# List entries of a routed expert loop loaded one step ahead and copied on the chip: one Trainium2 core, two-layer encoder with mixture of experts

## The reference

```python
for i in range(DEPTH):
    ...
    h = rmsnorm(x, norm_ffn_g[i])
    x = x + hierarchical_moe(h, ...)   # top-1 of 4 groups, top-2 of its 8 experts
...
def expert_block(args):
    xb, e = args                       # up to 128 tokens of expert e
    hid = jax.nn.silu(xb @ w_gate[e]) * (xb @ w_up[e])
    return hid @ w_down[e]
```

## Time and profile before

| | us |
|---|---|
| median of 3 runs | 2135.43 |
| lowest and highest of them | 2134.26, 2157.36 |
| the profiled execution, its own time | 2135.17 |
| span of the profiled execution | 2133.3 |

### The profile page before, as it was taken

How to read it: one execution, slowest core, us unless ns; L and a number is a source line. 1 busy time by engine, 2 the same in 40 slices (tenths; PEclk the granted TensorE clock), 3 DMA queues, 4 the chain that set the end, 5 groups by cost and what they waited for, 6 DMA issues and landing times.

```text
span 2133.3 us, 31870 instructions
## 1 busy us (share of the span) xinstructions
PE 2004.4 (94%) x9518; PEld 1668.4 (78%) x9518; DVE 1574.5 (74%) x1886; ACT 1360.6 (64%) x1734; POOL 284.7 (13%) x313
## 2 busy tenths in 40 slices
PE   7999999999979999999999969998799999999991
PEld 6888778888867888888888758887688888888871
DVE  4334453426558989999999866777799999999986
ACT  3442243434337888888888855315588888888873
POOL 1000000000031222122112100001312112222110
PEclk9999999999979999999999979998899999999996
DMA  7331223323367999999999964233989999999976
GB/s 281 99 99 69 80 86 101 93 88 128 139 197 286 368 363 381 384 391 370 379 379 379 367 244 162 99 149 129 276 331 377 379 380 383 376 379 388 395 296 254
DMA packets 166743, 560.12 MB, mean 263 GB/s; under 512 B 31472, under 2 KB 32720, under 8 KB 164512
## 3 DMA queue, kind: packets, MB, share of 16 engines
q1 hardware_dynamic: 138816, 510.72, 64.1%
q0 software_dynamic: 25424, 39.56, 5.3%
q10 hardware_dynamic: 2448, 9.14, 1.2%
HBM read 541.94 MB, written 51.97 MB: 278 GB/s over the span
## 4 chain that ended last, share of the span: by engine, by line
PE 48%; DMA 30%; issue 9%; DVE 6%; POOLq 3%; ACT 2%; POOL 2%; SPq 0%; ACTq 0%; DVEq 0%; PEldq 0%
DMA y_rows<-big,metas 17%; PE bank L572 15%; PE bank L573 15%; PE bank L574 15%; DMA metas<-lists 11%; POOLq L504 2%; PE bank L652 1%; POOL big L507 1%; DVE big L1333 1%; PE bank L800 1%; DVE w_lo L1325 1%; PE bank L641 1%; DVE big L1582 1%; DVE bank L1578 1%; DVE x_res L1352 1%
## 5 line engine op out<-in xcount | busy, mean ns | idle before, releaser
L572 PE MATMUL bank<-w_hi,a_hi 128*128 128x512 f32 x1944 | 773.3, 398 | 15.7 <-DVE w_lo L1325 9.3
L574 PE MATMUL bank<-w_hi,a_lo 128*128 128x512 f32 x1944 | 760.8, 391 | 0.0
L573 PE MATMUL bank<-w_lo,a_hi 128*128 128x512 f32 x1944 | 758.6, 390 | 0.0
L1325 DVE TENSOR_TENSOR w_lo<-raw,w_hi 128x1024 fp32r<-128x1024 f32 x372 | 452.8, 1224 | 358.7 <-ACT w_hi L947 337.5
L947 ACT ACTIVATE w_hi<-raw 128x1024 fp32r<-128x1024 f32 x372 | 393.0, 1060 | 453.9 <-PE bank L574 438.6
L1325 DVE TENSOR_TENSOR w_lo<-big,w_hi 128x1024 fp32r<-128x1024 f32 x530 | 620.8, 1220 | 28.8 <-ACT w_hi L947 21.3
L947 ACT ACTIVATE w_hi<-big 128x1024 fp32r<-128x1024 f32 x530 | 547.7, 1064 | 104.2 <-PE bank L574 98.8
L572 PEld LDWEIGHTS bank<-w_hi,a_hi 128*128 128x128 f32 x1944 | 367.0, 189 | 91.6 <-DVE w_lo L1325 12.2
L574 PEld LDWEIGHTS bank<-w_hi,a_lo 128*128 128x128 f32 x1944 | 366.1, 188 | 79.2
L573 PEld LDWEIGHTS bank<-w_lo,a_hi 128*128 128x128 f32 x1944 | 366.7, 189 | 72.3
L1325 DVE TENSOR_TENSOR a_lo<-bank,a_hi 128x512 fp32r<-128x512 f32 x227 | 147.6, 684 | 58.7 <-ACT a_hi L947 51.9
(11 more groups left out here) (185 smaller groups left out, 1606.4 us busy)
## 6 DMA issues: line engine op xcount, KB each, us to landing
big<-in_w_gate SPq DMA_DIRECT2D x260, 512.0 KB
big<-in_w_up SPq DMA_DIRECT2D x254, 512.0 KB, 6.7
raw<-in_w_down SPq DMA_DIRECT2D x244, 512.0 KB, 6.7
raw<-in_a_w_in SPq DMA_DIRECT2D x64, 512.0 KB, 3.9
raw<-in_a_w_out SPq DMA_DIRECT2D x32, 512.0 KB, 3.2
big<-y_rows SPq DMA_DIRECT2D x16, 1024.0 KB, 7.0
big<-in_w_down SPq DMA_DIRECT2D x16, 512.0 KB, 9.8
raw<-in_b_w_in SPq DMA_DIRECT2D x16, 512.0 KB, 4.2
```

The costliest lines, as they stand in the source:

```text
L572: pe.matmul(dst, left_hi, right_hi, start=first, stop=False)
L573: pe.matmul(dst, left_hi, right_lo, start=False, stop=False)
L574: return pe.matmul(dst, left_lo, right_hi, start=False, stop=last)
L1325: return nc.vector.tensor_tensor(dst, src, f32(hi), ALU.subtract)
```

## The change

`metas` stays, and two buffers of the same form, `ahead_g` and `ahead_s`, are put into columns of `cols` that held the bias of the first mixer. The DMAs load into these; a GpSimd `tensor_copy` of 128x4 int32 then fills `meta_g` or `meta_s`. The load for the gather of item i+2 is issued right behind the gather of item i+1; the load for the scaling of item i+1 is issued right behind the scatter of item i, and its copy is made when that scatter has landed. ACT waits for the copy instead of the DMA (the counts change from 16 per load to 1 per copy). Three more groups of edits only rename: `stored`, `table`, `xc_act`, `xc_dve` and `summed` become one semaphore for both layers, with counts that run on.

```diff
+        ahead_g, ahead_s = cols[:, 0:4].bitcast(I32), cols[:, 4:8].bitcast(I32)
...
+                def load_ahead(i, dst, landed):
+                    b = block_of(i)
+                    pool.dma_start(dst, lst[:, bass.ds(b, 1), :].rearrange("p b w -> p (b w)")).then_inc(landed, 16)
+
                 def gather(i):
 
-                    b = block_of(i)
                     pool.wait_ge(M.x_full, i)
                     waited()
-                    pool.dma_start(meta_g, lst[:, bass.ds(b, 1), :].rearrange("p b w -> p (b w)")).then_inc(M.meta_g, 16)
-                    pool.wait_ge(M.meta_g, 16 * (i + 1 - FIRST))
+                    pool.wait_ge(M.ahead_g, 16 * (i + 1 - FIRST))
+                    waited()
+                    nc.gpsimd.tensor_copy(meta_g, ahead_g).then_inc(M.meta_g, 1)
+                    pool.wait_ge(M.meta_g, i + 1 - FIRST)
                     waited()
                     gather_rows(0, xg, M.gathered)
 
-                def load_meta(i):
-                    b = block_of(i)
-                    pool.dma_start(meta_s, lst[:, bass.ds(b, 1), :].rearrange("p b w -> p (b w)")).then_inc(M.meta_s, 16)
+                def scale_by(i):
+
+                    pool.wait_ge(M.ahead_s, 16 * (i + 1))
+                    waited()
+                    nc.gpsimd.tensor_copy(meta_s, ahead_s).then_inc(M.meta_s, 1)
+                    pool.wait_ge(M.meta_s, i + 1)
+                    waited()
...
                 def scatter(i):
                     scatter_rows(i, meta_s, y_sb)
+                    load_ahead(i + 1, ahead_s, M.ahead_s)
                     pool.wait_ge(M.scattered, 16 * (i + 1))
                     waited()
+                    scale_by(i + 1)
...
-                load_meta(0)
+                load_ahead(0, ahead_s, M.ahead_s)
+                load_ahead(2, ahead_g, M.ahead_g)
+                scale_by(0)
                 load_gain(2 * L + 2, A["norm_mix_g"][1] if L == 0 else A["final_norm_g"])
                 gather(2)
...
+                load_ahead(3, ahead_g, M.ahead_g)
                 with pool.Fori(2, n - 1) as i:
                     gather(i + 1)
+                    load_ahead(i + 2, ahead_g, M.ahead_g)
                     scatter(i - 2)
-                    load_meta(i - 1)
                 scatter(n - 3)
-                load_meta(n - 2)
                 scatter_rows(n - 2, meta_s, y_sb)
                 scatter_rows(n - 1, meta_g, end_y)
...
-                    act.wait_ge(M.meta_s, 16 * (i + 1))
+                    act.wait_ge(M.meta_s, i + 1)
                     weighted_rows(y_sb, 2, meta_s)
```

More of the change, by code:

```diff
@@ L223, in encoder_trunk @@
         ROUTE = ["rw_ready", "x_t", "lg_full", "lg_read", "slots", "slot_oh", "first_full", "first", "weighted",
[L224 to L228, removed]
+                 "exps", "g_shifted", "e_shifted", "chosen", "ranked", "placed", "listed", "small", "second", "rows", "row_full", "table",
+                 "xc_act", "xc_dve", "summed"]
+        rt = sems("route", ROUTE, {"stored": HALVES})
+        MOE = ["hi", "lo", "used", "chain",
+               "meta_g", "ahead_g", "ahead_s", "gathered", "x_full", "x_hi", "x_lo", "silu", "hid",
                "h_full", "h_hi", "h_lo", "y_out", "meta_s", "scattered",
-               "added", "summed"]
-        m = [sems(f"moe{n}", MOE, {"raw": ROUND, "stored": HALVES}) for n in range(LAYERS)]
+               "added"]
+        m = [sems(f"moe{n}", MOE, {"raw": ROUND}) for n in range(LAYERS)]
         SU = 3 * 2 * KC
@@ L245, in copied @@
             if L == 0:
-                return m[L].xc_act, 2 * (t + 1)
-            return (m[L].xc_dve, 2 * (t + 1)) if t < HT else (m[L].xc_act, 2 * (t - HT + 1))
+                return rt.xc_act, 2 * (t + 1)
+            return (rt.xc_dve, 2 * (t + 1)) if t < HT else (rt.xc_act, 2 * TT + 2 * (t - HT + 1))
         block = ctx.enter_context(nc.Block())
@@ L326, in load_dn @@
                         .then_inc(landed if landed is not None else M.raw[GU + j], 16)
-                place_free = {0: lambda: sp.wait_ge(M.stored[0], 16),
-                              4: lambda: sp.wait_ge(M.stored[1], 16 * HT),
+                place_free = {0: lambda: sp.wait_ge(rt.stored[0], 16 * (L + 1)),
+                              4: lambda: sp.wait_ge(rt.stored[1], 16 * HT * (L + 1)),
                               5: lambda: sp.wait_ge(rt.first_full, HALVES * L + HALVES),
@@ L389, in moe @@
                 if L == 0:
-                    sp.wait_ge(M.table, 1)
+                    sp.wait_ge(rt.table, L + 1)
                     for grp in (2, 3):
@@ L863, in moe @@
                 h_transposes(1)
-                pe.wait_ge(M.table, 1)
+                pe.wait_ge(rt.table, L + 1)
                 n = pe.value_load(table[0:1, 0, TABLE - 1:TABLE], min_val=E - 2, max_val=ITEMS_MAX - 2) + 2
@@ L969, in raw_copy @@
                 for j in range(2):
-                    copy(xt[L][t][:, j * 512:(j + 1) * 512], bank[b + j][:, :]).then_inc(m[L].xc_act, 1)
+                    copy(xt[L][t][:, j * 512:(j + 1) * 512], bank[b + j][:, :]).then_inc(rt.xc_act, 1)
             def logits_copy(L, t, b):
@@ L1188, in moe @@
                         if L == 0:
-                            act.wait_ge(M.stored[1], 16 * HT)
+                            act.wait_ge(rt.stored[1], 16 * HT)
                             for i in range(4):
@@ L1214, in moe @@
                 round_(2, moe_raw, early_down)
-                act.wait_ge(M.table, 1)
+                act.wait_ge(rt.table, L + 1)
                 n = act.value_load(table[0:1, 0, TABLE - 1:TABLE], min_val=E - 2, max_val=ITEMS_MAX - 2) + 2
@@ L1232, in moe @@
                 act.wait_ge(M.used, ROUND * n + DN)
-                act.wait_ge(M.meta_g, 16 * (n - FIRST))
+                act.wait_ge(M.meta_g, n - FIRST)
                 weighted_rows(end_y, 4, meta_g)
@@ L1349, in add @@
                 dve.wait_ge(g.comb[t % COMBS], 16 * ((L * TT + t) // COMBS + 1))
-                nc.vector.tensor_tensor(two[:, 0, :], two[:, 0, :], two[:, 1, :], ALU.add).then_inc(M.summed, 1)
-                dve.wait_ge(M.summed, t + 1)
+                nc.vector.tensor_tensor(two[:, 0, :], two[:, 0, :], two[:, 1, :], ALU.add).then_inc(rt.summed, 1)
+                dve.wait_ge(rt.summed, TT * L + t + 1)
                 nc.vector.tensor_tensor(x_res[:, t, :], x_res[:, t, :], two[:, 0, :], ALU.add).then_inc(M.added, 1)
@@ L1731, in moe @@
                 round_(2, moe_raw, early_down)
-                dve.wait_ge(M.table, 1)
+                dve.wait_ge(rt.table, L + 1)
                 n = dve.value_load(table[0:1, 0, TABLE - 1:TABLE], min_val=E - 2, max_val=ITEMS_MAX - 2) + 2
```

14 lines of the change are left out of this document (7 added, 7 removed).

## The result

| us | before | after |
|---|---|---|
| median | 2142.22 (2132.96 to 2157.6, 15 runs) | 2123.56 (2119.72 to 2130.76, 15 runs) |
| profiled execution, span | 2133.3 | 2117.8 |

The medians lie 18.7 us apart, the two profiles 15.5 us.

A forecast was written before the change was run, and what follows sets the result against it. PE's own work was taken as the bound at 17.80 us a round, with stalls from late list entries on top. Terms -7.3, -4.6 and -2.1 summed to -14.0 us, from 2135.17 to 2121.2 us; range 2116 to 2131.

The forecast's parts named there:

- PE's own work takes 17.80 us a round, and the excess over it is what can be won: Expert-stage rounds in both layers: PE sets 17.80 us a round; only the stalls beyond that can go.
- -7.3, -4.6 and -2.1: Stalls expected to go, in us: layer 0's rounds, layer 1's rounds, and layer 1's tail behind the last x transposes.
- What is late first is meta_s: POOL's string ahead of `y_out`: the load of `meta_s` has 0.3 us of cover; moving it gives 7 us.
- pays only by making POOL's loop shorter ... PE gains nothing more from that: Load of `meta_g` a round ahead: takes 5.2 us off POOL's string, adds a copy, gives PE nothing more.
- the 3.16 us of issue: Late issue on POOL in layer 0's longest stall, with a scatter of 8.37 us; expected to fit the new cover.
- Room of POOL, about 6 us a round: POOL's loop after the change: 11.5 us and two copies against 17.80, so POOL waits about 6 us for `y_out`.
- Copies of 0.2 us, 0.3 with their wait: Two GpSimd copies of 128x4 a round: 0.2 us each, 0.3 with wait, 0.98 at most, hidden in POOL's idle time.
- DVE pays nothing: DVE beside the copies: 1.2 us free a round, 0.4 lost at 0.2 per copy, so cost taken as 0.
- Ahead of layer 1's loop, 0 between -1.5 and +2: New order of loads, copy, gain and gather before layer 1's loop: taken as 0, ends -1.5 and +2 us.
- Rival A: Copies held for whole DVE runs make POOL's loop 21.5 us: +215 us, 2336 us; chance 0.04.
- Rival B: Copies cost DVE more than its 1.2 us free a round: 2136 us, at the end 2167; chance 0.11.
- Rival C: Small load queued behind the scatter's packets, `meta_s` there at 22.9 us, half the gain: 2128 us; chance 0.08.

The follow-up runs named there:

- e1: Changed kernel with only the scaling's entries loaded ahead, the gather loading its own as before: ratio to the kernel before 0.9999, median 2145.87 us.
- e2: Changed kernel with only the gather's entries loaded ahead, the scaling's loaded behind the landed scatter: ratio to the kernel before 0.9922, median 2128.61 us.
- e8: Changed kernel with eight GpSimd memsets of 128x1024 ahead of each gather in layer 1's loop: its items 3 to 31 took 653.7 us against 498.4.
- e7: Changed kernel with four GpSimd memsets of 128x1024 ahead of each gather in layer 1's loop: its items 3 to 31 took 499.5 us against 498.4.
- e4: Changed kernel with eight more GpSimd copies of 128x4 a round, four ahead of each copy: ratio to the kernel before 0.9939, median 2134.25 us.

## Why the prediction was right or wrong

The forecast was 2121.2 us, 14.0 below the profiled execution of 2135.17, and the median of the changed kernel is 2123.56, inside the range. The profiles differ by 15.5 us, the ratio's interval gives 13 to 23. That the time itself came so near is in part luck: the forecast started near the median of three runs, 2135.43, and by 15 runs it is 2142.22; 14.0 below that would be 2128.2.

- *PE's own work takes 17.80 us a round, and the excess over it is what can be won:* right to the hundredth. -7.3, -4.6 and -2.1 came as they were summed, since no stall is left, and no round from item 3 on falls below 17.79.
- *"What is late first is meta_s", and the gather's load ahead "pays only by making POOL's loop shorter ... PE gains nothing more from that":* this step failed, though the sum did not show it. I had given the gather until 17.8 us and had not set its landing against that. e1 shows that when only `y_out` is relieved the gather takes over as what is late, and the timed runs gain nothing; e2 shows that the shorter string alone removes every stall. What was right in it is the arithmetic of the string, and the sentence that it happens to be as long as PE's round. That it "wanders" was the smaller part: most of the stalls stand behind the 3.16 us of issue, which the prediction had seen once and counted as the longest late case.
- *Room of POOL, about 6 us a round:* of the right size. In the changed kernel's round POOL idles 2.88 and 4.71 us. The sum had the scatter at 7.6 us, where it took 5.7, and the copies at 0.6 with their waits, where they took 1.7. 4.4 us of memsets are hidden and use the room up, as the scatter lands later with them; 8.9 are not.
- *Copies of 0.2 us, 0.3 with their wait:* a copy alone takes 0.18, but in the loop it took 1.13 (ahead of the gather) and 0.59 (behind the scatter) by the median. The prediction's sentence on the Trainium skill had this: by the page "SBUF — State Buffer" (Who interferes with whom) a VectorE instruction with two SBUF inputs contends with a GpSimd instruction that reads SBUF, and the later one is blocked for the whole of the other. The traces agree: the longest copy is 1.29 us, 1.1 more than one alone, and a subtraction takes 1.2. It was hidden in POOL's idle time, as reckoned there.
- *DVE pays nothing:* right. It is busy for 93.38 of 100 us against 93.29 and 93.58, as the window of the changed kernel shows (columns as above):

```profile
800.00:900.00 100.00, 100.00 (x472) 83.39 (x471) 93.38 (x90) 86.85 (x103) 27.45 (x33) 1.00 1.00 383
```

- *Ahead of layer 1's loop, 0 between -1.5 and +2:* x transposes of item 2 behind those of item 1 went from 21.02 to 20.11, -0.9 in this pair. The other profiles have 22.17 and 21.81 before, 20.35 after.
- *Rival A (POOL becomes the bound):* didn't come about, but the mechanism is real; e8 built it. It decides from a little over 4.4 us more per round on, since e7 leaves POOL no idle time. *Rival B (DVE pays):* no, not even with ten copies a round. *Rival C (half of the gain, the load queued behind the scatter):* the entries land behind the scatter, the copy starts 15.6 us behind the x transposes, and there is cover.
- *What the sum left out:* the medians differ by 18.7 us. 14.1 of them are the forecast's three terms as the profiles have them; 1.4 are the small pieces outside them; the other 3.2 are that the profiled execution of before lies 7.05 us below the median of its runs and that of after 3.84 below its own. The three profiles of the kernel before, at or below the medians of the runs beside them, don't show where a slower run has those 3 us. That stays open.

## What to carry to other kernels

Where an engine issues a string of DMAs that wait for each other, add up the string and set it against the round of the engine that bounds: at equal length it costs little in ordinary rounds, turns a single late issue into a stall (10.8 to 12.3 us of 13 to 15 here), and can be the whole of what is to be won; a microsecond more in every round costs several. Such a string has more than one deadline; relieve the one that the waits name, and the next one takes over (e1), while a shorter string relieves all of them at once (e2). If two distant marks of the bound engine lie an exact multiple of its best round apart, the stretch between them has no stall left to remove.

## What the runs showed that I had not expected

- A GpSimd copy that reads SBUF ends with VectorE's instruction. The copy shown in the changed kernel's round starts at 1866.83 and takes 1.13 us; the timeline of DVE there:

```profile
1863.96 3.95 DVE L1339 TENSOR_TENSOR w_lo<-raw,w_hi 128x1024 fp32r<-128x1024 f32 x3
```

DVE's run of three ends at 1867.91, the copy at 1867.96. In the 115 of 124 copies that took over 0.25 us this distance is 34 to 48 ns. The gather goes out 3.4 to 3.7 us behind the x transposes in every round of layer 1's loop, so the copy ahead of it meets DVE at nearly the same point each time; its median is 1.13 us.

- The scatter lands in 5.7 us by the median instead of 7.6 when it is issued 6.4 us behind the gather instead of 1.36; in e2 it was 5.9, in e1, where it follows the gather closely again, 7.5. Within e7 it is 5.8 in layer 0 (6.4 us apart) and 7.9 in layer 1 (2.1 apart). The gather's own landing gains less: 5.7 us after, 6.3 in the second profile of before and 7.0 in e1. The distance isn't all of it: in e4 the two are 5.2 to 5.9 us apart, and the scatter lands in 7.2, the gather in 7.1.
- The 3.16 us of issue near the end of each layer are still there after the change, ahead of the 149th and the 300th DMA that POOL issues; 2.67 us of them show as its idle time. In the changed kernel's timeline:

```profile
1159.62 1.02 POOL L539 DMA_INDIRECT y_rows<-big,metas  x1 [4.55 <-ACT big L1173]
1163.31 0.55 POOL L515 DMA_DIRECT2D cols<-lists  x1 [2.67 <-issue]
1168.08 0.73 POOL L532 COPY metas<-cols 128x4 int32<-128x4 int32 x1 [4.21 <-DMA cols<-lists]
```

It now falls into the scatter's flight and costs nothing. What it is that takes 3.16 us there is not shown.
